# Up projection of the second FFN kind: 15 of 22 units in two PSUM banks with 512-column products

## The reference, cut to what matters

```python
def conv_ffn(h, w_up, ffn_dw_w, ffn_dw_b, w_down):
    val, gate = jnp.split(h @ w_up, 2, axis=-1)
    gate = causal_dwconv(gate, ffn_dw_w, ffn_dw_b)
    return (jax.nn.silu(gate) * val) @ w_down
```

## Time and profile before

| | us |
|---|---|
| median of 3 runs | 2067.23 |
| lowest and highest | 2066.44, 2067.92 |
| the profiled execution | 2066.47 |
| its span | 2064.7 |
| TensorE busy | 2051.9 (99%) |
| VectorE busy | 1678.1 (81%) |
| ScalarE busy | 1060.8 (51%) |
| GpSimd busy | 248.8 (12%) |

### The profile page before, as it was taken

The page is one execution under the profiler, slowest core; times in us unless marked ns, Lnnn a source line. Parts: engine busy times, 40 slices in busy tenths (PEclk is TensorE's granted clock), DMA queues, the critical chain, the costliest instruction groups (busy, mean ns, idle before and its releaser), DMA issues.

```text
span 2064.7 us, 36780 instructions
## 1 busy us (share of the span) xinstructions
PE 2051.9 (99%) x15426; PEld 1962.7 (95%) x15426; DVE 1678.1 (81%) x2490; ACT 1060.8 (51%) x1290; POOL 248.8 (12%) x176
## 2 busy tenths in 40 slices
PE   9999999999999999999999999999999999999998
PEld 9999999899999989979989999999988999989997
DVE  8888897888789788898996668677798996758775
ACT  6887354456755434355545445434346445445442
POOL 0212065000006500001201001100000300000110
PEclk9999999999999999999999999999999999999999
DMA  7553555554245455544554445545544554535543
GB/s 266 195 190 137 186 183 186 175 214 151 103 144 184 158 200 209 184 159 148 204 184 180 167 144 183 178 169 206 184 171 150 190 184 183 184 132 178 182 166 119
DMA packets 58292, 361.82 MB, mean 175 GB/s; under 512 B 6736, under 2 KB 9360, under 8 KB 21136
## 3 DMA queue, kind: packets, MB, share of 16 engines
q1 hardware_dynamic: 58128, 359.48, 49.3%
HBM read 358.37 MB, written 1.08 MB: 174 GB/s over the span
## 4 chain that ended last, share of the span: by engine, by line
PE 96%; DVE 2%; ACT 1%; issue 0%; DMA 0%; POOL 0%; SPq 0%; DVEq 0%; ACTq 0%
PE acc L637 68%; PE acc L646 11%; PE acc L636 7%; PE acc L768 1%; PE acc L766 1%; PE acc L767 1%; DVE w_lo L1196 1%; PE acc L971 1%; PE pA L1020 1%; ACT w_hi L2066 0%; DMA raw<-in_wide 0%; PE pC L814 0%; PE pB L1044 0%; PE pD L1131 0%; PE pB L1106 0%
## 5 line engine op out<-in xcount | busy, mean ns | idle before, releaser
L637 PE MATMUL acc<-in_both,w_hi 128*128 128x256 f32 x7408 | 1346.6, 285 | 2.8 <-issue 1.5
L637 PEld LDWEIGHTS acc<-in_both,w_hi 128*128 128x128 f32 x7408 | 1156.9, 192 | 8.1 <-issue 4.3
L637 PE MATMUL acc<-in_both,w_lo 128*128 128x256 f32 x4656 | 1147.8, 283 | 0.1
L1196 DVE TENSOR_TENSOR w_lo<-raw,w_hi 128x2048 fp32r<-128x2048 f32 (+1 forms) x349 | 757.9, 2174 | 134.7 <-ACT w_hi L2066 133.9
L637 PEld LDWEIGHTS acc<-in_both,w_lo 128*128 128x128 f32 x4656 | 831.6, 192 | 5.0 <-POOL in_both L2676 0.4
L2066 ACT CAST w_hi<-raw 128x2048 fp32r<-128x2048 f32 (+1 forms) x349 | 630.2, 1807 | 228.2 <-PE acc L637 142.9
L2676 POOL TENSOR_TENSOR in_both<-arena,in_both 128x256 fp32r<-128x256 f32 (+1 forms) x112 | 119.5, 1067 | 1206.9 <-ACT in_both L2528 508.3
L646 PE MATMUL acc<-in_both,w_hi 128*128 128x512 f32 x952 | 227.9, 392 | 0.0
L646 PEld LDWEIGHTS acc<-in_both,w_hi 128*128 128x128 f32 x952 | 175.5, 188 | 34.0
L1847 DVE SCALAR_TENSOR_TENSOR arena<-arena,cols 128x256 f32<-128x256 f32 x480 | 200.5, 490 | 0.0
L2686 POOL TENSOR_TENSOR arena<-arena 128x256 f32<-128x256 f32 x44 | 96.4, 2192 | 376.2 <-ACT arena L2349 376.2
(11 more groups left out here) (289 smaller groups left out, 1528.0 us busy)
## 6 DMA issues: line engine op xcount, KB each, us to landing
raw<-in_wide SPq DMA_DIRECT2D x285, 1024.0 KB, 4.8
raw<-in_narrow SPq DMA_DIRECT2D x64, 704.0 KB, 4.0
arena<-cs_rows SPq DMA_DIRECT2D x16, 256.0 KB, 4.8
arena<-in_mem SPq DMA_DIRECT2D x3, 1024.0 KB, 6.9
x<-in_x SPq DMA_DIRECT2D x4, 256.0 KB, 6.3
raw<-in_wide SPq DMA_DIRECT2D x2, 512.0 KB, 5.5
tables<-in_tables SPq DMA_DIRECT2D x1, 1024.0 KB, 16.8
arena<-cs_rows SPq DMA_DIRECT2D x16, 64.0 KB, 5.4
```

The costliest lines, as they stand in the source:

```text
L637: return mm(outs[m], w[:, k, at], moving[:, c, :], start=start, stop=stop)
L1196: tt(w_lo[g % RAW][:, 0:n], raw[g % RAW][:, 0:n], w_hi[g % HI][:, 0:n], ALU.subtract).then_inc(lo_ready, 1)
```

## The change

In both `up_b` projections units 4 to 18 are multiplied in a new way, with two banks each. `two_banks` picks the pair: for unit 4 the banks of units 0 and 1, for unit 5 those of units 2 and 3, and so on by turns. Bank `m` takes tile `m`: its left half is the sum over the high input, its right half the sum over the low input. The products are 16 of 512 columns (`w_hi` x `in_both`, L654 in the new file) and 16 of 256 (`w_lo` x `in_hi`, L661). From unit 4 on TensorE waits for `acc_free` of `g - 1`, which is the release of unit `u - 2` and all before it.

For these units ScalarE copies the right halves of both banks to a buffer `f_b` in SBUF (L2449), VectorE adds the left halves to them (L1731) and raises `acc_free`, and takes the taps from `f_b` instead of the bank. GpSimd multiplies silu and value (L2787) and ScalarE writes the high part one unit later. The weights are split three units ahead instead of two.

```diff
+TWO_FROM, TWO_TO = 4, 19
...
+        def two_banks(seg, u):
+
+            pair = (seg.base + 3) % 4 // 2 ^ 1 ^ u % 2
+            return acc[2 * pair], acc[2 * pair + 1]
...
+                    elif seg.name == "up_b" and j >= TWO_FROM:
+                        pe.wait_ge(acc_free, g - 1)
                     elif not pair and g >= 4:
                         pe.wait_ge(acc_free, u + (seg.base - 3))
...
-                    if side_by_side(seg.name, j, seg.units):
+                    if seg.name == "up_b" and TWO_FROM <= j < TWO_TO:
+                        banks = two_banks(seg, j)
+
+                        def both_inputs(m, ks):
+                            for k in ks:
+                                ins = mm(banks[m][:], hi[:, k, m * P:(m + 1) * P], in_both[:, seg.chunk0 + k].rearrange("p a l -> p (a l)"),
+                                         start=k == 0, stop=k == nk - 1)
+                            return ins
+                        for m in range(2):
+                            both_inputs(m, range(1))
+                        for m in range(2):
+                            for k in range(nk):
+                                mm(banks[m][:, 0:T], lo[:, k, m * P:(m + 1) * P], in_hi[:, seg.chunk0 + k, :], start=False, stop=False)
+                        for m in range(2):
+                            last = both_inputs(m, range(1, nk))
...
+                    def halves_added(u):
+                        banks, f = two_banks(seg, u), f_b[:, u % 2]
+                        for m in range(2):
+                            dve.wait_ge(side_b, 2 * ((TWO_TO - TWO_FROM) * l + u - TWO_FROM) + m + 1)
+                            ins = tt(f[:, m, :], f[:, m, :], banks[m][:, 0:T], ALU.add)
+                            E.mark(ins) if m == 0 else ins.then_inc(acc_free, 1)
+
+                    for u in range(TWO_FROM):
+                        first(u)
+                        if u == 1:
+                            scale_unit(seg, nth, 2)
+                        if u < TWO_FROM - 1:
+                            split(u + 4, seg, u + 4)
+                        second(u)
+                    for u in range(TWO_FROM, TWO_TO):
+                        halves_added(u)
+                        dve.wait_ge(acc_free, seg.base + u + 1)
+                        taps(u, f_b[:, u % 2, 1])
+                        E.passed(silu_ready, 1)
+                        split(u + 3, seg, u + 3)
+                    for u in range(TWO_TO, seg.units):
+                        first(u)
+                        if u < seg.units - 1:
+                            split(u + 3, seg, u + 3)
+                        second(u)
...
+                    def side(u):
+                        act.wait_ge(unit_done, seg.base + u + 1)
+                        for m in range(2):
+                            copy(f_b[:, u % 2, m, :], two_banks(seg, u)[m][:, T:2 * T]).then_inc(side_b, 1)
...
+                    for u in range(TWO_FROM, TWO_TO):
+                        side(u)
+                        split(u + 3, seg, u + 3)
+                        if u > TWO_FROM:
+                            E.wait(hid_ready)
+                            high(u - 1)
+                        silu(u)
...
+                    pool.wait_ge(silu_ready, 16 + GROUPS_S + n * FC + 8 * (n - 1) + u + 1)
+                    pool.wait_ge(acc_free, u + (seg.base + 1))
+                    pool.wait_ge(gin_ready, u + (made["hid"][n] - 1))
+                    tt(f_h[:, j % 2, :], f_s[:, j % 2, :], f_b[:, j % 2, 0, :], ALU.mult).then_inc(hid_ready, 1)
```

More of the change, by code:

```diff
@@ L272, in build @@
         f_g, f_v, f_s, f_h = (view(512 * n, 2, T) for n in range(4))
+        f_b = view(4096, 2, 2, T)
         kq_t = view(0, ATT_G * (ATT_KV + ATT_H), T)
@@ L402, in build @@
         side_a = sem("side_a")
+        side_b = sem("side_b")
         gated_v = sem("gated_v")
@@ L637, in product @@
                         return mm(outs[m], w[:, k, at], moving[:, c, :], start=start, stop=stop)
-                    if side_by_side(seg.name, j, seg.units):
+                    if seg.name == "up_b" and TWO_FROM <= j < TWO_TO:
[12 more added lines that the diff above has]
+                            last = both_inputs(m, range(1, nk))
+                    elif side_by_side(seg.name, j, seg.units):
                         begins, ends = not (pair and j % 2), not pair or j % 2 == 1
@@ L1678, in run, with taps @@
                     hid0 = made["hid"][2 + l]
-                    def first(u, j, banks):
-                        g = taps3(f_g[:, j % 2, :], banks[1], lambda t: wcol(f"f_conv{l}", u * FFN_TAPS + t),
+                    nth = 5 + 3 * l
+                    seg = take("up_b")
+                    def taps(u, gate):
+                        g = taps3(f_g[:, u % 2, :], gate, lambda t: wcol(f"f_conv{l}", u * FFN_TAPS + t),
                                   wcol(f"f_bias{l}", u), conv_ready)
@@ L1686, in first, with second @@
                                 E.settle()
-                    def second(u, j, banks):
+                    def first(u):
+                        if u < EARLY:
+                            dve.wait_ge(early_v, scaled_units(nth) + u + 1)
+                        dve.wait_ge(unit_done, seg.base + u + 1)
+                        taps(u, banks_of(seg.base + u)[1])
+                    def second(u):
                         E.wait(silu_ready)
                         dve.wait_ge(gin_ready, u + (hid0 - 1))
-                        tt(f_h[:, j % 2, :], f_s[:, j % 2, :], banks[0], ALU.mult).then_inc(acc_free, 1)
-                    project("up_b", first, second, steps={v_order: 2, silu_ready: 1}, between=True, nth=5 + 3 * l, behind=8, at=7)
+                        tt(f_h[:, u % 2, :], f_s[:, u % 2, :], banks_of(seg.base + u)[0], ALU.mult).then_inc(acc_free, 1)
+                    def halves_added(u):
[22 more added lines that the diff above has]
+                        second(u)
                     E.passed(inh_ready, FC)
@@ L2372, in run, with silu, high, used @@
                     norm()
-                    base = take.base()
-                    project("up_b", hidden(lambda u: act.wait_ge(acc_free, u + (base + 1))), steps={conv_ready: 1},
-                            nth=5 + 3 * l, behind=8)
+                    seg = take("up_b")
+                    def silu(u):
+                        E.wait(conv_ready)
+                        fn(f_s[:, u % 2, :], f_g[:, u % 2, :], ACT.Silu).then_inc(silu_ready, 1)
+                    def high(u):
+                        copy(in_hi[:, u + DC, :], f_h[:, u % 2, :]).then_inc(inh_ready, 1)
+                    def used(u):
+                        silu(u)
+                        act.wait_ge(acc_free, seg.base + u + 1)
+                        high(u)
+                    def side(u):
+                        act.wait_ge(unit_done, seg.base + u + 1)
+                        for m in range(2):
+                            copy(f_b[:, u % 2, m, :], two_banks(seg, u)[m][:, T:2 * T]).then_inc(side_b, 1)
+                    for u in range(TWO_FROM):
+                        if u < TWO_FROM - 1:
+                            split(u + 4, seg, u + 4)
+                        used(u)
+                    for u in range(TWO_FROM, TWO_TO):
[4 more added lines that the diff above has]
+                            high(u - 1)
+                        silu(u)
+                    E.wait(hid_ready)
+                    high(TWO_TO - 1)
+                    for u in range(TWO_TO, seg.units):
+                        if u < seg.units - 1:
+                            split(u + 3, seg, u + 3)
+                        used(u)
                     project("down")
@@ L2686, in multiply, with multiply_sum @@
                     tt(f_h[:, j % 2, :], f_s[:, j % 2, :], f_v[:, j % 2, :], ALU.mult).then_inc(hid_ready, 1)
+                def multiply_sum(u, j):
+                    if not TWO_FROM <= u < TWO_TO:
+                        return
+                    pool.wait_ge(silu_ready, 16 + GROUPS_S + n * FC + 8 * (n - 1) + u + 1)
+                    pool.wait_ge(acc_free, u + (seg.base + 1))
+                    pool.wait_ge(gin_ready, u + (made["hid"][n] - 1))
+                    tt(f_h[:, j % 2, :], f_s[:, j % 2, :], f_b[:, j % 2, 0, :], ALU.mult).then_inc(hid_ready, 1)
                 def run():
@@ L2691, in run @@
                     low_parts(name, piece["hid"][n], lambda u: bass.ds(u + DC, 1), lambda u, j: f_h[:, j % 2].unsqueeze(1),
-                              multiply if name == "up_a" else None)
+                              multiply if name == "up_a" else multiply_sum)
                     skip("down")
```

## The result

The changed kernel takes 2082.48 us (median of 4 runs, 2082.04 to 2082.95) against 2066.88 for the kernel before on the same chip: a ratio of 1.0075, 95% interval 1.0062 to 1.0087. That is 15.6 us slower. The span of its profiled execution is 2080.3 us, where it was 2064.7.

What follows compares the result with a forecast made beforehand. TensorE, busy 99% of the span, was taken as the bound. From the profiled 2066.47 us, - 5.8 (products) + 17.7 (stalls) + 3.9 (clock) gave 2082.3, and 0.76 for the median made 2083.0; range 2078 to 2087.5.

Steps and rivals of the forecast that it cites:

- The likeliest case: Whole kernel: cheaper products, two stalls before unit 4 and two cold clock starts give 2083.0 us; chance 0.62.
- Step 1: Two-bank units of up_b: one 512-column product for two of 256 saves 0.012 us a pair, 5.8 us less.
- Step 2: Before unit 4 in both up_b: TensorE idles 8.8 us until unit 2 is free, 17.7 us more in all.
- Step 3: After each unit 4 stall: TensorE's clock falls and a cold start costs 1.95 us, 3.9 us more in all.
- Step 4: Settled two-bank units of up_b: copies, adds and GpSimd's second operation hide within 5.57 us a unit, costing nothing.
- the kept clock: Rival, stalls before unit 4: the clock stays up through them, 3.9 us less, 2079.1 us; chance 0.12.
- the late clock: Rival, after the stalls: up to 5 instead of 1.95 us each, typically 2086.5 us; 0.15 shared with a slow engine loop.
- products without gain: Rival, two-bank units: 512-column products no faster than two of 256, 5.8 us more, 2088.8 us; chance 0.06.
- the missing stall: Rival, before unit 4: unit 2 is free when unit 4 is due, so no stall, 2061.4 us; chance 0.03.
- The loop over ScalarE and GpSimd: Rival, settled two-bank units: these engines bind, 2 us slip a stage, typically 2086.5 us; 0.15 shared with slow clock recovery.

Runs made afterwards that it cites:

- the run with narrow products: Changed kernel with two products of 256 columns for each of 512, same banks, waits, copies and additions: 2088.93 us, ratio 1.0107.
- the run with the wait alone: Kernel before with one edit, unit 4 of both up_b waiting until units 0, 1 and 2 are free: 2088.55 us, ratio 1.0105.
- filling the stall: Changed kernel with 36 products of ones by ones ahead of unit 4's wait in both up_b, keeping TensorE busy: 2078.30 us, ratio 1.0054.
- the run with two units free: Changed kernel with unit 4 waiting only for units 0 and 1, whose banks it takes, not unit 2: 2072.39 us, ratio 1.0027.

## Why the prediction was right

I had said 2083.0 us; it is 2082.48. The likeliest case came about, by the steps it was made of. Most of the half microsecond between them is the starting point: the sum started from 2067.23, and beside the changed kernel the kernel before took 2066.88. The added time was 15.8 by the sum and is 15.6.

Step 1, the products. Said: 0.012 us a pair and 5.8 us, unit 5.57. Measured: 5.57, and 6.4 us by the run with narrow products, 5.9 by the run with the wait alone, 5.6 to 6.0 by the trace. The 0.228 us read from one-bank products in `down` holds for a unit with two banks. The single products that I subtracted, 0.28 and 0.39 us, are in none of the rows that I pointed at; the first is in the changed kernel's timeline above, the second is the mean of all 952 wide products at L646 in the trace before. The rule of the Trainium skill that I weighed ("TensorE: Matmul & The Clock Gate", "Back-to-back issue gap"), with 1.2 us, falls short by a factor of five here: products of 256 columns come 0.120 us apart in this kernel, not 0.109. The same section calls this rule the gap of an isolated product, and gives 131 ns for 512 columns in a stream of weight loads and products; I had left that out, and the 0.228 us of this trace don't bear it out either.

Step 2, the stall. Said: 8.8 us twice, released by VectorE's product for unit 2. The row is 8.81 us with that releaser, in both projections, and the wait by itself brings it about in the kernel before.

Step 3, the clock. Said: 3.9 us for two falls, from the program's first microseconds. Measured 4.2 by filling the stall, 3.6 by the length of unit 4 in the trace. That the sum fits so well is in part luck: I took the early pace as 1.9 times slower, but the products of this kernel with 256 columns come 0.213 us apart at the low level and 0.120 at the high one, 1.8 times. The two starts were not alike either, 2.1 and 1.4 us over a full-pace unit. And the rows at the program's beginning show a slow pace, not a low clock: the granted clock reads 1.00 there in this profile, so that the lower level at that end was my inference. The changed kernel's trace shows it directly, with 0.50 in the row behind the stall. The Trainium skill's statement (same page, "Part 1: The HAM clock gate") that the idle state is the throttled one is borne out by the row with the clock at 0.50 behind the stall.

Step 4, the settled part. Said: hidden, with half a microsecond to spare on VectorE. Right that it is hidden; VectorE is idle for 1.13 us a unit, of which I had named 0.45 as the wait for the first copy and 0.5 as spare. I expected at most one of GpSimd's operations to be slow, and one is, the low part (2.61 us, against 0.74 before), which costs nothing.

Of the rivals, the kept clock is excluded by the rows and by the filled stall, the late clock by unit 4's length (2.1 us over, not 5), products without gain by the run with narrow products, and the missing stall by the rows. The loop over ScalarE and GpSimd does not bind: units come at TensorE's pace.

One thing I had not seen. I wrote that nothing short of a count that runs ahead could avoid the stall. That is so for two-bank units from unit 4. But the count asked for one unit more than the banks need, and this alone was worth 10 us; and two banks from unit 8, with the count corrected and two splits moved, have no stall at all. Both could have been read from the trace before. In the earlier trace rows unit 1 is free at 1259.20, 4.9 us ahead of unit 2. And VectorE waits for TensorE for the first time ahead of unit 8:

```profile
1284.28 0.55 DVE L1636 TENSOR_SCALAR arena<-acc,cols 128x256 f32<-128x256 f32 x1 [0.54 <-PE acc L637]
```

## What to carry to other kernels

Two banks a unit in place of one halve the depth of the ring. When you spend buffers on a faster producer, ask at the start of the stage, not in its settled part, how far the consumer is behind: its lag there was covered by a ring of four. With a ring of two it cost a stall of 3.9 us a stage, and of 8.8 with a count that asked for one unit too many. Start such a scheme at the unit where the consumer has caught up, and count for each wait which buffer it needs.

## What the runs showed of the hardware that I had not expected

A gap of 3.9 us was enough for the clock to fall, with the same low level behind it as after 8.8 us: in the run with two units free, TensorE then worked 5 us at 0.50. Unit 4 took 7.9 and 7.8 us there in place of 5.57, so the slow start was 2.3 us on top of the 3.9. Only some 0.7 of the 2.3 were lost in the end, by an estimate from the same rows, because the slow unit hid a wait of 1.6 us.

One product of ones by ones with plain float32 operands, 128 columns, is two records 0.112 us apart (72 for 36 products in 8.20 us), while the kernel's rounded operands give one record each.
